# mLSTM heads in row form: denominators as rows, M and m spread by split products

## What is computed

```python
a_inter = b + m_state[..., None]
d = where(causal, b[..., :, None] - b[..., None, :] + lic[..., None, :], -inf)
m_t = maximum(a_inter, max(d, axis=-1))
scores = einsum('bhtd,bhsd->bhts', qc, kc) * exp(d - m_t[..., None])
den = w_inter * einsum('bhd,bhtd->bht', n_state, qc) + sum(scores, axis=-1)
h = num / maximum(abs(den), exp(-m_t))[..., None]
...
h = layernorm32(h, LN_EPS)        # over the 256 columns of a head, eps 1e-5
```

## Time and profile before

| | |
|---|---|
| median of the runs | 1939.55 us |
| the profiled execution | 1945.08 us |
| its span in the trace | 1943.0 us |
| mean granted TensorE clock | 0.988 |
| TensorE busy | 1903.3 us |
| VectorE, ScalarE, GpSimd busy | 1032.3, 783.0, 240.5 us |

### The profile page before, as it was taken

One profiled execution on the slowest core, in us unless ns is written; L12 is line 12 of the kernel. 1 busy time (PEld: TensorE's weight loads), 2 busy tenths in 40 slices (PEclk: granted clock), 3 DMA queues, 4 the chain that ended last, 5 costly groups with the idle time before them and its releaser, 6 DMA issues.

```text
span 1943.0 us, 21345 instructions
## 1 busy us (share of the span) xinstructions
PE 1903.3 (98%) x8752; PEld 1571.7 (81%) x8752; DVE 1032.3 (53%) x1297; ACT 783.0 (40%) x1046; POOL 240.5 (12%) x264
## 2 busy tenths in 40 slices
PE   7999999999999999999999999999989999999997
PEld 5788888878888888888888888888877888888885
DVE  6444434347354666564444334655564877774345
ACT  4332322236443555433223222555554444443234
POOL 5000001201300111140000022100003100000212
PEclk9999999999999999999999999999989999999998
DMA  4423232342241222422222332312213232323331
GB/s 146 163 89 106 87 108 88 105 153 92 76 141 60 93 76 82 137 97 98 98 98 97 98 98 97 111 64 68 74 44 103 82 109 87 108 88 109 98 104 59
DMA packets 51074, 188.98 MB, mean 97 GB/s; under 512 B 6345, under 2 KB 6345, under 8 KB 50081
## 3 DMA queue, kind: packets, MB, share of 16 engines
q1 hardware_dynamic: 46224, 166.74, 26.0%
q0 software_dynamic: 4176, 19.83, 3.0%
q10 hardware_dynamic: 576, 1.05, 0.1%
HBM read 179.18 MB, written 11.03 MB: 98 GB/s over the span
## 4 chain that ended last, share of the span: by engine, by line
PE 95%; DVE 3%; ACT 1%; issue 0%; DMA 0%; DVEq 0%; ACTq 0%; POOLq 0%
PE psum L1675 95%; DVE xl L1090 1%; DVE wl L1093 1%; PE psum L2027 0%; DMA cols<-in_cols 0%; ACT at L766 0%; ACT wh L766 0%; DVE x L1087 0%; DVE az L1090 0%; DVE R L1125 0%; DVE at L1446 0%; DVE fta L1087 0%; DVE tm L1331 0%; ACT R L766 0%; DVE xl L1093 0%
## 5 line engine op out<-in xcount | busy, mean ns | idle before, releaser
L1675 PE MATMUL psum<-xh,wh 128*128 128x512 f32 x1760 | 697.1, 396 | 14.8 <-DVE xl L1090 11.6
L1675 PE MATMUL psum<-xl,wh 128*128 128x512 f32 x1760 | 687.7, 391 | 0.0
L1675 PE MATMUL psum<-xh,wl 128*128 128x512 f32 x1760 | 687.5, 391 | 0.0
L1093 DVE TENSOR_TENSOR wl<-wraw,wh 128x1024 fp32r<-128x1024 f32 (+1 forms) x313 | 405.4, 1303 | 388.1 <-ACT wh L766 387.5
L766 ACT ACTIVATE wh<-wraw 128x1024 fp32r<-128x1024 f32 (+1 forms) x313 | 325.7, 1050 | 382.1 <-PE psum L1675 380.1
L1675 PEld LDWEIGHTS psum<-xh,wh 128*128 128x128 f32 x1760 | 332.1, 189 | 94.5 <-issue 22.6
L1675 PEld LDWEIGHTS psum<-xl,wh 128*128 128x128 f32 x1760 | 332.1, 189 | 70.1 <-issue 2.9
L1675 PEld LDWEIGHTS psum<-xh,wl 128*128 128x128 f32 x1760 | 331.9, 189 | 70.1
L1539 POOL TENSOR_TENSOR ssq<-x 128x512 f32<-128x512 f32 x6 | 6.2, 1039 | 717.3 <-DVE x L1173 454.0
L1675 PE MATMUL psum<-wh,xh 128*128 128x512 f32 (+1 forms) x256 | 88.2, 344 | 0.4 <-ACT zv L766 0.4
L1675 PE MATMUL psum<-wh,xl 128*128 128x512 f32 (+1 forms) x256 | 86.0, 336 | 0.0
(11 more groups left out here) (299 smaller groups left out, 2245.7 us busy)
## 6 DMA issues: line engine op xcount, KB each, us to landing
wraw<-in_w_ffn SPq DMA_DIRECT2D x87, 512.0 KB, 3.3
wraw<-in_w_down SPq DMA_DIRECT2D x44, 512.0 KB, 3.3
...
```

Of the source, the lines that this page charges most:

```text
L1093: return e.tensor_tensor(dst, src, hi.bitcast(F32), ALU.subtract)
L1675: return e.matmul(dst, lhsT, rhs, start=start, stop=stop, skip_group_check=skip)
```

## The change

- A step H.m is put ahead of H.0: TensorE spreads m of the head into bank 2, ScalarE writes exp(-2m) ("em", 128 x 512) from it, and H.0 on TensorE waits for that before it spreads M into the same bank. Both spreads are fp32r products over 36 rows: rows 0 to 3 hold the high parts of M and m, rows 32 to 35 the rests, and `sel` has ones in both places. A step Q5 writes these rows; `sel` and the zero rows are set up in `ws`.
- The denominators become rows: `onesr` (128 x 128 ones) is the stationary operand and the scores are moved, so that the sum stands on all partitions (eight products of 512, 384, 256 and 128 columns).
- ScalarE squares them (times 256e-5), VectorE takes the maximum with em times 256e-5 ("dd").
- The norm works on the undivided numerator: T.5 is one product with ones over 512 columns, T.6 adds dd to the sum of squares and takes the power -1/2 as logarithm and exponential on 128 x 512, T.7 multiplies. The old T.7, T.8 and T.9 are gone, and so are the reciprocals and the square root on 128 x 4.
- The places of steps change: for head 0, H.0 to H.6 come a quarter later each; H.m of heads 1, 2 and 3 stands behind quarters (105, 3), (113, 3) and (121, 3); the merges G0, G1, G2 and G4 come earlier.
- Scratch rows of the gates move into `mg`, which is free then; the memory as a whole is as large as before.

The diff, cut (semaphore tables and renamed scratch rows left out):

```diff
@@ -39,21 +39,23 @@
 GATE_AT = {
     (74, 0): "L0 L1 L2 L3", (74, 2): "Q0", (74, 3): "L4 L5 L6", (75, 1): "L7", (75, 2): "Q1",
     (75, 3): "L8 L9 L10", (76, 1): "Q2", (77, 1): "L11 L12 L13", (77, 3): "L14", (78, 0): "Q3", (78, 1): "Q4",
-    (78, 3): "L15", (80, 1): "L16",
+    (78, 3): "L15 Q5", (80, 1): "L16",
     (81, 3): "V0", (83, 3): "V1", (85, 3): "V2", (87, 3): "V3", (89, 3): "V4 V5 V6 V7",
 }
 MIX_AT = {
-    (102, 0): "H0.0", (102, 1): "H0.1 H0.2 H0.3", (102, 2): "H0.4", (102, 3): "H0.5 H0.6", (103, 1): "H0.7",
-    (103, 2): "T0.0", (103, 3): "T0.1", (104, 0): "T0.2", (105, 3): "T0.3 T0.4", (106, 0): "H1.0",
+    (102, 0): "H0.m", (102, 1): "H0.0", (102, 2): "H0.1 H0.2 H0.3", (102, 3): "H0.4", (103, 0): "H0.5 H0.6",
+    (103, 1): "H0.7", (103, 2): "T0.0", (103, 3): "T0.1", (104, 0): "T0.2", (105, 3): "T0.3 T0.4 H1.m",
+    (106, 0): "H1.0",
     (106, 1): "H1.1 H1.2", (107, 2): "H1.3 T0.5", (107, 3): "H1.4 T0.6", (108, 3): "H1.5", (109, 0): "T0.7",
-    (109, 1): "H1.6", (110, 0): "T0.8", (110, 1): "H1.7 T0.9", (110, 3): "T0.10 G0 G1 T1.0", (111, 0): "T1.1",
-    (111, 1): "T1.2 T1.3", (111, 2): "T1.4", (111, 3): "T1.5", (112, 0): "T1.6", (114, 0): "H2.0 T1.7",
-    (114, 1): "H2.1 H2.2", (115, 2): "H2.3 T1.8 H2.4", (115, 3): "T1.9 H2.5", (116, 2): "T1.10 G2",
+    (109, 1): "H1.6", (109, 3): "G0 G1", (110, 1): "H1.7", (110, 3): "T1.0", (111, 0): "T1.1",
+    (111, 1): "T1.2 T1.3", (111, 2): "T1.4", (111, 3): "T1.5", (112, 0): "T1.6", (113, 3): "H2.m",
+    (114, 0): "H2.0 T1.7", (114, 1): "H2.1 H2.2", (115, 2): "H2.3 H2.4", (115, 3): "H2.5 G2",
     (116, 3): "H2.6", (117, 3): "G3 H2.7", (118, 0): "T2.0", (118, 3): "T2.1", (119, 0): "T2.2", (119, 1): "T2.3",
-    (119, 2): "T2.4", (119, 3): "T2.5", (120, 0): "T2.6", (122, 0): "H3.0 T2.7", (122, 1): "H3.1 H3.2",
-    (123, 2): "H3.3 T2.8 H3.4", (123, 3): "T2.9 H3.5", (124, 2): "T2.10 G4", (124, 3): "H3.6", (125, 3): "G5 H3.7",
+    (119, 2): "T2.4", (119, 3): "T2.5", (120, 0): "T2.6", (121, 3): "H3.m", (122, 0): "H3.0 T2.7",
+    (122, 1): "H3.1 H3.2",
+    (123, 2): "H3.3 H3.4", (123, 3): "H3.5 G4", (124, 3): "H3.6", (125, 3): "G5 H3.7",
     (126, 0): "T3.0", (126, 3): "T3.1", (127, 0): "T3.2", (127, 1): "T3.3", (127, 2): "T3.4", (127, 3): "T3.5",
-    (128, 0): "T3.6", (129, 0): "T3.7", (129, 2): "T3.8", (129, 3): "T3.9 T3.10 G6 G7",
+    (128, 0): "T3.6", (129, 0): "T3.7", (129, 3): "G6 G7",
...
     vh = sb("vh", [128, 4, 1024], F32R, mix)
     vl = sb("vl", [128, 4, 1024], F32R, mix)
-    rows = sb("rows", [4, 4, 512], F32, mix)
-    sel = sb("sel", [4, 4, 128], F32, mix)
+    rows = sb("rows", [4, 2, 512], F32, mix)
+    rowr = sb("rowr", [36, 2, 512], F32R, mix)
+    sel = sb("sel", [36, 4, 128], F32R, mix)
     tmpm = sb("tmpm", [128, 4, 512], F32, mix)
     ccol = sb("ccol", [128, 32], F32, mix)
...
 
         return tmpm[:, i, :] if i < 4 else tm2[:, i - 4, :]
+
+    def em(h):
+
+        return (R1 if h % 2 else ssg)[:, :]
 
     def quad(ap):
...
@@ -886,9 +893,10 @@
                     act(ra, ra, ACT.Exp, scale=-1.0).then_inc(gate_a.sem, 1)
                     e.wait_ge(*gate_a.at("exp"))
                     act(ra, ra, ACT.Ln, bias=1.0).then_inc(gate_a.sem, 1)
-                elif i == 4:
-                    e.wait_ge(*gate_d.at("cc"))
-                    act(ccol[:, 16:32], bank(6)[:, 16:32], ACT.Exp, scale=-1.0).then_inc(gate_a.sem, 1)
+                elif i == 5:
+                    e.wait_ge(*gate_d.at("m"))
+                    e.wait_ge(*sel_d.at("rowz"))
+                    act(rowr[0:4, :, :], rows[:, :, :], ACT.Copy).then_inc(gate_a.sem, 1)
             elif kind == "zuev":
                 j, = a
                 u, g = us[:, j % 5, :], us[:, 5, :]
@@ -920,7 +928,12 @@
                     scale=rc[:, i:i + 1]).then_inc(v_a.sem, 1)
             elif kind == "H":
                 h, s = a
-                if s in (1, 2):
+                if s == "m":
+                    e.wait_ge(*h_p.at(h, "m"))
+                    if h >= 2:
+                        e.wait_ge(*t_d.at(h - 2, "u"))
+                    act(em(h), bank(2), ACT.Exp, scale=-2.0).then_inc(h_a.sem, 1)
+                elif s in (1, 2):
                     for j in (2 * s - 2, 2 * s - 1):
                         e.wait_ge(*h_p.at(h, "M"))
                         act(att[:, OFF[j]:OFF[j] + 512 - 128 * j], bank(2)[:, 128 * j:512], ACT.Exp,
@@ -931,8 +944,9 @@
                         act(sh[:, r], att[:, r], ACT.Copy).then_inc(h_a.sem, 1)
                 elif s == 7:
                     e.wait_ge(*h_p.at(h, "den"))
-                    act(rcs[:, h % 2, :], bank(2)[:, 0:8].rearrange("p (i z) -> p i z", z=2)[:, :, 0],
-                        ACT.Abs).then_inc(h_a.sem, 1)
+                    if h:
+                        e.wait_ge(*t_d.at(h - 1, "n1"))
+                    act(tm(5), bank(2), ACT.Square, scale=256e-5 ** 0.5).then_inc(h_a.sem, 1)
                     e.wait_ge(*h_p.at(h, "num"))
                     e.wait_ge(s_spill, 16)
                     act(hn[:, 2 * h, :], bank(0), ACT.Copy).then_inc(h_a.sem, 1)
@@ -945,12 +959,10 @@
                     e.wait_ge(*t_d.at(h, "c1"))
                     act(tm(4), hn[:, 2 * h + 1, :], ACT.Square).then_inc(t_a.sem, 1)
                 elif s == 6:
-                    c2 = rcs[:, 2 + h % 2, :]
-                    e.wait_ge(*t_d.at(h, "v1"))
-                    act(c2, c2, ACT.Sqrt, bias=eps5[:, 0:1]).then_inc(t_a.sem, 1)
-                elif s == 9:
-                    e.wait_ge(*t_p.at(h, "sp"))
-                    act(tm(4), bank(7), ACT.Copy).then_inc(t_a.sem, 1)
+                    e.wait_ge(*t_d.at(h, "u"))
+                    act(tm(5), tm(5), ACT.Ln, scale=1.0 / 256).then_inc(t_a.sem, 1)
+                    e.wait_ge(*t_a.at(h, "ln"))
+                    act(tm(5), tm(5), ACT.Exp, scale=-0.5).then_inc(t_a.sem, 1)
             elif kind == "ogev":
                 j, = a
...
@@ -1192,8 +1204,16 @@
                 low(wsl[:, :], wsr[:, :], wsh[:, :]).then_inc(ws_d.sem, 1)
                 for k in range(8):
                     e.tensor_scalar(wif[:, k, :], wif[:, k, :], col("gmix", k), None, ALU.mult).then_inc(ws_d.sem, 1)
+
+                e.wait_ge(*mix_g.at("zero"))
+                sel2 = sel[:, :, :].rearrange("p h t -> p (h t)")
+                e.tensor_copy(sel2, mg[0:36, 4, :]).then_inc(sel_d.sem, 1)
+                e.tensor_copy(rowr[:, :, :], mg[0:36, 4:6, :]).then_inc(sel_d.sem, 1)
+                e.wait_ge(*sel_d.at("zero"))
+                e.tensor_copy(sel2[0:4, :], mg[0:4, 3, :]).then_inc(sel_d.sem, 1)
+                e.tensor_copy(sel2[32:36, :], mg[0:4, 3, :]).then_inc(sel_d.sem, 1)
             elif kind == "gmm":
-                ri, rf = rows[:, 0, :], rows[:, 1, :]
+                ri, rf = mg[0:4, 2, :], mg[0:4, 0, :]
                 e.wait_ge(*gate_p.at("mm"))
                 e.wait_ge(*rs_a.at("gmix", "R"))
...
@@ -1222,6 +1242,9 @@
                 elif i == 4:
                     e.wait_ge(*gate_p.at("tr"))
                     e.tensor_copy(ccol[:, 0:16], bank(6)[:, 0:16]).then_inc(gate_d.sem, 1)
+                elif i == 5:
+                    e.wait_ge(*gate_a.at("rh"))
+                    low(rowr[32:36, :, :], rows[:, :, :], rowr[0:4, :, :]).then_inc(gate_d.sem, 1)
             elif kind == "ln":
                 i, = a
...
@@ -1302,20 +1325,15 @@
                         e.wait_ge(*h_a.at(h, "s", i))
                         low(sl[:, r], att[:, r], sh[:, r]).then_inc(h_d.sem, 1)
                 elif s == 7:
-                    cc = rcs[:, h % 2, :]
                     e.wait_ge(*h_p.at(h, "num"))
                     e.wait_ge(s_spill, 16)
                     e.tensor_copy(hn[:, 2 * h + 1, :], bank(1)).then_inc(h_d.sem, 1)
-                    e.wait_ge(*h_a.at(h, "abs"))
-                    e.wait_ge(*gate_a.at("em"))
-                    e.tensor_tensor(cc, cc, ccol[:, 16:32].rearrange("p (i h) -> p i h", h=4)[:, :, h],
-                                    ALU.max).then_inc(h_d.sem, 1)
-                    e.wait_ge(*h_d.at(h, "max"))
-                    e.reciprocal(cc, cc).then_inc(h_d.sem, 1)
+                    e.wait_ge(*h_a.at(h, "em"))
+                    e.wait_ge(*h_a.at(h, "d"))
+                    stt(em(h), em(h), 256e-5, tm(5), ALU.mult, ALU.max).then_inc(h_d.sem, 1)
             elif kind == "T":
                 h, s = a
                 h0, h1, t4, bD = hn[:, 2 * h, :], hn[:, 2 * h + 1, :], tm(4), bank(7)
-                cc, c2 = rcs[:, h % 2, :], rcs[:, 2 + h % 2, :]
                 if s == 0:
                     e.wait_ge(*h_a.at(h, "h0"))
                     e.wait_ge(*h_d.at(h, "h1"))
@@ -1331,21 +1349,12 @@
                     e.tensor_tensor(t4, t4, tm(5), ALU.add).then_inc(t_d.sem, 1)
                 elif s == 6:
                     e.wait_ge(*t_p.at(h, "cs"))
-                    e.wait_ge(*h_d.at(h, "rec"))
-                    stt(c2, bD[:, 0:4], 1.0 / 256, cc, ALU.mult, ALU.mult).then_inc(t_d.sem, 1)
```

(71 more changed lines are left out.)

15 lines of the change are left out of this document (7 added, 8 removed).

## The result

The changed kernel takes **1974.72 us** (median of four runs, 1973.48 to 1976.59) against 1938.88 for the kernel before in the same comparison (four runs, 1938.01 to 1939.7): ratio 1.0181, 95% interval 1.0168 to 1.0193. It is slower by 35.8 us; the forecast was slower, at 1965.4 within 1953 to 1977. Its profiled execution took 1974.28 us, with a span of 1972.6 and a mean granted clock of 0.982.

What follows compares the result with a forecast made beforehand. TensorE, busy for 98% of the span, was taken as the bound. Added 40.5 us less saved 14.7 gave net +25.8 on the profiled 1945.08, 1970.9; less 5.5 for the median, 1965.4 us, range 1953 to 1977.

Steps and rivals of the forecast that it cites:

- The round trip: At H.0 TensorE waits for ScalarE's em: 2.4 us on head 0, 9.0 on head 1, 11.1 each on heads 2 and 3.
- The waits at H0.7 and the set-up: 1.3 us waiting for head 0's lower halves of the scores; 0.5 us for copies ahead of the diagonal of R.
- The spread of M: Two split products at 0.23 us each replace a float32 spread of 1.05 us on each head: 2.4 us saved.
- The denominators and T.8: Row-form denominators save 0.87 us per head, 3.5; dropping the float32 spread of the reciprocal deviation saves another 3.5.
- T1.5: The 0.60 us wait before it, from VectorE late beside G0 and G1, goes as these come earlier: 0.6 us saved.
- The clock behind waits: Half clock after TensorE stands: 5.1 us lost behind the three long waits, 0 taken behind the 2.4 us wait.
- The clock at the numerators: The clock drop at denominators and numerators of heads 0, 2 and 3 goes: 1.56 us, three times, 4.7 saved.
- it is 5.5 above the median: The profiled 1945.08 us lies 5.5 above the runs' median, 1939.55; so 1970.9 for the changed kernel becomes 1965.4.
- TensorE is not held: Rival at H.0: em ready within 1.4 us, only savings and two small waits remain, 1926.7 us; chance 0.04.
- The clock stays low for longer: Rival: after each of the four waits the clock stays low longer, 6.8 us more, 1972; chance 0.10.
- The row form does not lift the clock: Rival: what follows the denominators, not their two columns, made the clock fall; 4.7 us more, 1970; chance 0.08.
- Table loads cost more: Rival: emptying ScalarE before six loads on the waits costs as much again, 7.7 us more, 1973; chance 0.02.

Runs made afterwards that it cites:

- T0.6 back: The "em late" version with T0.6 and T0.7 at the changed kernel's places, (107, 3) and (109, 0): 1936.86 us, ratio 0.9988.
- em late: Changed kernel with m in bank 7, H.m behind its head's exponentials, head 0's steps at old places, T0.6 and T0.7 behind H1.6: 1933.26 us, ratio 0.9968.
- both repeats: The kernel before, unchanged, profiled twice more: 1939.85 and 1940.94 us, against 1945.08 in the first profile.
- the 128-row fillers: Changed kernel plus unread 128-row products into bank 7 ahead of H.0's wait, 36 on head 1, 45 on heads 2 and 3: 1969.28 us, ratio 1.015.
- the last one: The "em late" version with T1.6 and T2.6 behind the next head's exponentials, their T.7 and H.m of heads 2 and 3 moved too: 1929.92 us, ratio 0.9948.

## Why the prediction was right, and where its sum was not

**The round trip: right.** The step that decided was "TensorE waits for that at H.0, in order". The waits came at 2.1, 8.7, 10.8 and 10.7 us over the pitch for 2.4, 9.0, 11.1 and 11.1 in the sum, released by ScalarE's exponential each time. That it is the place and not the work is shown: em moved ahead or put into another bank takes the long waits away, and with them all of the loss. Together the four waits were 1.3 us shorter than forecast (32.3 for 33.6).

**The waits at H0.7 and the set-up: right**, at 1.4 (1.3) and 0.5 (0.5).

**A wait that the sum did not have: H1.7, 2.2 us.** The prediction followed T1.6's logarithm and exponential into the wait of head 2, but not T0.6's into head 1's scores. VectorE's lower halves before, then ScalarE, VectorE and GpSimd after:
```profile
658.04 1.55 DVE L1093 TENSOR_TENSOR sl<-att,sh 128x512 fp32r<-128x512 f32 x2
```
```profile
665.53 1.28 ACT L769 ACT_TABLE_LOAD   x1 [2.87 <-DVE tm L1102]
666.83 1.30 ACT L773 ACTIVATE tm<-tm 128x512 f32<-128x512 f32 x2
668.03 1.04 ACT L773 ACTIVATE wh<-wraw 128x1024 fp32r<-128x1024 f32 x1
668.98 1.35 ACT L773 ACTIVATE sh<-att 128x512 fp32r<-128x512 f32 x2
...
672.45 1.29 DVE L1099 TENSOR_TENSOR x<-x,tm 128x512 f32<-128x512 f32 x2
673.66 2.62 DVE L1105 TENSOR_TENSOR sl<-att,sh 128x512 fp32r<-128x512 f32 x2
...
673.89 1.57 POOL L1626 TENSOR_TENSOR tm<-tm,x 128x512 f32<-128x512 f32 x1 [26.73 <-DVE x L1099]
```
ScalarE waits 2.87 us for VectorE's addition, loads a table, and does both passes before it comes to the weight pass and the high part of the scores; VectorE's lower half ends at 676.28, and H.7 starts at 676.33. Before, the lower half ended 3.0 us ahead of H.7 (659.59 against 662.60); after, 2.15 behind its place (674.13, one pitch after 673.90), so it is 5.2 later. By the rows 3.5 of these are T0.6 on ScalarE, which delays the weight pass and the high part of the scores; 0.6 are T0.7, now two passes on VectorE where one stood; 1.1 are the lower halves themselves, slow beside G0, which T0.7 releases. Any one alone would leave a wait of 0.5 us at most. "T0.6 back" against "em late" shows that the place of T0.6 and T0.7 makes the wait; the three shares are read from the trace, not tried one by one.

**The spread of M: wrong, nothing saved.** The prediction took 0.23 us for a 36-row split product and 0.53 as its upper bound. Without a wait it holds the next start off by 0.43 (632.91 to 633.34), the product behind it by 0.33 instead of 0.23, and its own start comes 0.32 after the one ahead instead of 0.23: 0.62 more in all than without it, above that bound, and 1.24 for two of them. The float32 spread, read the same way, was also 1.24: pitches of 0.31, 1.05 and 0.34, less two ordinary ones. The 2.4 us were read from one pitch in place of three.

**The denominators and T.8: right**, 3.5 each: 1.33 (heads 0 and 1) and 1.21 (heads 2 and 3) for 2.15; T.8's 0.87 goes on each head, and the new T.5 costs what the old one did (with the product behind it 1.09, 658.27 to 659.36, for 1.13, 645.82 to 646.95 before). **T1.5**: its wait is gone, 0.6; whether through the earlier G0 and G1, as forecast, was not tried by itself.

**The clock behind waits: mis-sized.** 6.4 for the three long waits, where 5.1 was taken, and 1.5 behind head 0's, where 0 was taken out of 0 to 1.7: half clock began at 600.5 us, and the six weight products behind head 0's H.0 took 2.72 us.

**The clock at the numerators: right in kind, wrong in size.** In the profiles taken here, the row form had full clock on 29 of 32 heads, and the three others are head 1 behind the 2.4 us wait at H1.7 (three of the six profiles with that wait); the column form lost it on 8 of 16. What in the column form makes the clock fall on one head and not on another is open. The 4.7 us, three heads, came from the one execution in which it was lost three times; both repeats lost it twice, 3.1.

**The sum.** Measured terms added: 32.3 (em) + 1.4 + 2.2 + 0.5 + 6.4 + 1.5 = 44.3, where 40.5 was forecast. Saved: 3.5 + 3.5 + 0.6 + 4.7 = 12.3, where 14.7 was. Net +32.0 against the first profile. The trace can be asked directly: from head 0's first spread to the end of head 3's numerators it is 187.44 us before (597.27 to 784.71) and 219.28 after (596.27 to 815.55), +31.8; head 3's T.8 saves another 0.9 later, and the part of the program ahead of the mix was 1.0 shorter, which is within the scatter: in its three profiles the kernel before starts the mix at 597.27, 596.57 and 597.90. So against its own execution the forecast (+25.8) was 3.4 low: 1974.28 - 1945.08 = 29.2. By its terms it was 6.2 low (32.0 for 25.8); the 2.8 between the two are the early start and small differences that no run explains, so that much of the agreement is luck.

**The base.** The other 5.9 of the 9.3 us by which 1974.72 lies above 1965.4 is the step "it is 5.5 above the median". The 5.5 were taken off as if the changed kernel's ordinary execution were as much shorter as the old one's. But 1.5 us in the first profile are head 0's drop, already counted as saved, and 3.4 are the drop at 1243 us, which the changed kernel's profile shows too (the row at 1272.90). Why that one comes in some executions and not in others is open; with the 128-row fillers the profiled execution, without it, took 1965.42 us and the three others, of which no profile was taken, 1969.25 to 1969.73.

**The rivals.** "TensorE is not held" fell; its 1926.7 needs the waits gone and all the savings real, and the nearest run to that, the last one, took 1929.92. "The clock stays low for longer" holds in part, 2.8 of its 6.8 us. "The row form does not lift the clock" fell: four stretches at 1.00. "Table loads cost more" fell: on head 1 the load starts 0.02 us after the pass ahead of it ends (640.50 + 1.13 = 641.63, 641.65), and the pass behind it 0.02 after the load's end (641.65 + 1.28 = 642.93, 642.95). The prediction looked only at the room behind the load, while its rival spoke of emptying the engine ahead of it. The Trainium skill ("ScalarE: Activation LUTs", What ACT_TABLE_LOAD costs) gives about 2.66 us for a switch with its drain; these rows, 1.32 us from pass to pass, do not agree with it.
